# A transformer layer on one core: a later subtraction in the projection, and compression's first loads ahead of the phase boundary

## What is computed

```python
h = x * (1.0 + sc_m) + sh_m
q_a, kvc, kvs, kvw, g_a, p_b, q_c, k_c, v_c, g_mrg = _split(h @ lp['w_in'], IN_SPLITS)
kvc_full = jnp.concatenate([paged_rows(past['nsa_cmp'], past['page_table']), kvc], axis=3)
kc = compress_rows(kvc_full[:, 0], lp['phi_w1'][0], lp['phi_pe'][0], lp['phi_w2'][0])
def compress_rows(rows, w1, pe, w2):
    hid = lax.conv_general_dilated(rows, w1, (CMP_STRIDE,), 'VALID', ...)
    hid = jax.nn.gelu(hid + jnp.einsum('ld,ldh->h', pe, w1))
    return (hid @ w2).reshape(B, G, -1, dk)
```

## Time and profile before

| what | value |
|---|---|
| device time, median of 3 runs | 1933.16 us (1930.5 to 1934.42) |
| the profiled execution, own time | 1922.61 us |
| its span | 1920.8 us |
| TensorE busy | 1722.9 us (90%) |
| VectorE busy | 1100.5 us (57%) |
| ScalarE busy | 569.5 us (30%) |
| GpSimd busy | 425.6 us (22%) |

### The profile page before, as it was taken

One profiled execution on the slowest core, in us unless ns is written; L12 is line 12 of the kernel. 1 busy time (PEld: TensorE's weight loads), 2 busy tenths in 40 slices (PEclk: granted clock), 3 DMA queues, 4 the chain that ended last, 5 costly groups with the idle time before them and its releaser, 6 DMA issues. The chain is left out here.

```text
span 1920.8 us, 38852 instructions
## 1 busy us (share of the span) xinstructions
PE 1722.9 (90%) x16171; PEld 1506.5 (78%) x16171; DVE 1100.5 (57%) x1937; ACT 569.5 (30%) x1216; POOL 425.6 (22%) x525
## 2 busy tenths in 40 slices
PE   4999888988989995999998997777899999999998
PEld 1898778887988994999986454554797999999776
DVE  3214676677665433899974555364586544444456
ACT  1235433333222321343433665222553200000000
POOL 0000910000001303232312779544100000000500
PEclk7899999998999997999997999898999999999999
DMA  5547774353444766665653852567574233333231
GB/s 230 158 127 208 183 230 147 108 175 106 156 145 160 241 213 224 216 217 186 219 147 131 308 141 83 170 232 250 182 215 147 77 88 89 88 88 135 88 98 70
DMA packets 241285, 311.14 MB, mean 162 GB/s; under 512 B 41557, under 2 KB 192493, under 8 KB 235222
## 3 DMA queue, kind: packets, MB, share of 16 engines
q1 hardware_dynamic: 211862, 176.72, 30.0%
q0 software_dynamic: 29248, 131.93, 21.2%
HBM read 281.19 MB, written 79.61 MB: 188 GB/s over the span
## 5 line engine op out<-in xcount | busy, mean ns | idle before, releaser
L302 PE MATMUL inp_acc<-hh,inp_wh 128*128 128x272 f32 (+1 forms) x1072 | 340.1, 317 | 20.8 <-DVE inp_wl L274 18.8
L302 PE MATMUL inp_acc<-hl,inp_wh 128*128 128x272 f32 (+1 forms) x1072 | 316.2, 295 | 0.0
L302 PE MATMUL inp_acc<-hh,inp_wl 128*128 128x272 f32 (+1 forms) x1072 | 316.0, 295 | 0.0
L302 PEld LDWEIGHTS inp_acc<-hh,inp_wh 128*128 128x128 f32 (+1 forms) x1072 | 207.1, 193 | 36.2 <-DVE inp_wl L274 19.3
L274 DVE TENSOR_TENSOR inp_wl<-inp_w,inp_wh 128x1024 fp32r<-128x1024 f32 (+1 forms) x67 | 81.2, 1212 | 233.6 <-ACT inp_wh L455 233.2
L302 PEld LDWEIGHTS inp_acc<-hl,inp_wh 128*128 128x128 f32 (+1 forms) x1072 | 208.3, 194 | 3.4 <-issue 3.1
L302 PEld LDWEIGHTS inp_acc<-hh,inp_wl 128*128 128x128 f32 (+1 forms) x1072 | 207.6, 194 | 0.4
L563 POOL DMA_DIRECT2D out_dram<-in_cache_dil_dram x84 | 42.8, 514 | 519.2 <-PE inp_acc L302 498.5
L1410 PE MATMUL cmp_pH<-cmp_RTh,cmp_w1h 128*128 128x256 f32 (+1 forms) x512 | 150.1, 293 | 3.4 <-issue 3.4
L269 DVE CAST trk_wh<-trk_w 128x1024 fp32r<-128x1024 f32 x62 | 46.4, 749 | 180.3 <-PE trk_pz L283 124.2
L1410 PE MATMUL cmp_pH<-cmp_RTl,cmp_w1h 128*128 128x256 f32 (+1 forms) x512 | 147.2, 287 | 0.4 <-issue 0.4
(11 more groups left out here) (597 smaller groups left out, 3805.5 us busy)
## 6 DMA issues: line engine op xcount, KB each, us to landing
inp_w<-in_w_in_dram SPq DMA_DIRECT2D x66, 512.0 KB, 6.1
trk_w<-in_w_ffn_dram SPq DMA_DIRECT2D x66, 512.0 KB, 3.9
out_dram<-in_cache_dil_dram POOLq DMA_DIRECT2D x64, 511.0 KB, 5.5
sdi_kv<-in_cache_dil_dram SPq DMA_DIRECT2D x288, 64.0 KB
ringA<-in_w_ada_dram SPq DMA_DIRECT2D x16, 1024.0 KB, 7.5
PT<-inp_o SPq DMA_DIRECT2D x58, 272.0 KB, 4.7
ada_wada<-in_w_ada_dram SPq DMA_DIRECT2D x8, 1024.0 KB, 17.6
out_dram<-in_cache_dil_dram POOLq DMA_DIRECT2D x16, 508.0 KB, 8.2
```

What stands on the lines that cost most here:

```text
L302: i = pe.matmul(out, l, r, start=(first and n == 0), stop=(last and n == 2))
```

## The change

Three edits. (1) In the projection, DVE's low part of tile n stands at 2.5 eighths of tile n-1 in the plan, where it stood 0.4 eighths before it. This moves it for n from 15 on. (2) Page numbers, row indices, the first three work items' pages, the keys' first-stage weights and the position code are fetched inside the projection's block, into memory that the recurrence has left (`retired` waits until its last state steps are done). With this, cache piece 1 of the dilated scores goes behind the 24 small DMAs, and SP waits for the pages of work items 3 and 4 before these 24; clearing `sdi_new` on DVE goes behind the first low parts. (3) The position code is split into high and low parts as up to 4 extra columns of the first sequence's windows (256 to 259), so that `hidden(0)` and `hidden(2)` compute its product as columns 256 and 258; ACT copies that column into the bias. The 64 matmuls, two transposes and three DVE copies go.

```diff
     def vector(self, dve):
         for n, (c, t, rows) in enumerate(self.tiles):
-            yield self.at(n - 1, -0.4) if n else self.at(0) - 0.9
+            yield self.at(n - 1, 2.5) if n else self.at(0) - 0.9
...
+    def early_sync(self, sp):
+        yield -15
+        sp.dma_start(m["pages"][:, :], a["page_lanes"]).then_inc(m["pages_in"], 16)
+        sp.dma_start(m["lane"][:, :], a["c_lane"]).then_inc(m["pages_in"], 16)
+        yield start_of(5) + 18
+        self.retired(sp)
+        sp.dma_start(m["first_w1"][:, :, :], w1[:, 0]).then_inc(m["w1_in"], 16)
+        sp.dma_start(m["first_pe"][:, :], ...).then_inc(m["w1_in"], 16)
+    def early_vector(self, dve):
+        yield start_of(5) - 2
+        dve.wait_ge(m["pages_in"], 32)
...
+    def early_pool(self, pool):
+        yield start_of(5) + 19
+        self.retired(pool)
+        pool.wait_ge(self.m["pages_ready"], 4)
+        for w in range(3):
+            gather_pages(pool, self.a, self.m["pageidx"], self.m["first_pages"][:, (w + 2) % 4], self.m[f"got{w}"], 0, w)
...
-            nw = self.nwin(s) + 1
+            nw = 258 + w if w in (0, 2) else self.nwin(s) + 1
...
-            if w == 0:
-                yield 0.15
-                pe.wait_ge(self.pek, 1)
-                for v in range(2):
-                    pe.wait_ge(self.w1in[v], 16)
-                    for c in range(16):
-                        i = pe.matmul(pK[0:1, 0, v * P:(v + 1) * P], self.peT[:, v * 16 + c:v * 16 + c + 1], self.w1[:, v, c, :], ...)
...
         self.load(sp, 0)
-        self.load(sp, 1)
         sp.wait_ge(self.zeroed, 1)
+        for w in (3, 4):
+            sp.wait_ge(self.cmp.got[w], 32)
...
-        for i in range(2, len(self.order)):
+        for i in range(1, len(self.order)):
```

More of the change, by code:

```diff
@@ L587, in start_of, with gather_pages @@
     return PROLOGUE + ITER * t
+def gather_pages(pool, a, idx, dst, got, s, c):
+    src = a["cache_nsa_cmp"][0].rearrange("n v g (c l) d -> (n v g c) (l d)", l=16)
+    for h in range(2):
+        pool.indirect_dma_start(
+            out=dst[:, h, :], out_offset=None, in_=src,
+            in_offset=bass.IndirectOffsetOnAxis(ap=idx[:, c, 2 * s + h:2 * s + h + 1], axis=0),
+        ).then_inc(got, 16)
 class Mixer:
@@ L1312, in __init__ @@
         self.pK = ps("pK", [P, 2, 512])
-        (self.wfree, self.loaded, self.idx, self.ix, self.pet, self.pek, self.hcd, self.hck, self.turned, self.high,
+        (self.wfree, self.loaded, self.idx, self.ix, self.pet, self.pek, self.hck, self.turned, self.high,
          self.kept, self.hd, self.act, self.od, self.ok) = (sem(s) for s in (
[L1315 to L1318, removed]
+             "wfree", "loaded", "idx", "ix", "pet", "pek", "hck", "turned", "high", "kept", "hd", "act", "od", "ok"))
+        self.w1in = sem("w1in")
+        self.got = [m[f"got{i}"] if i < 3 else sem(f"got{i}") for i in range(self.NR)]
         self.gotp = [sem(f"gotp{i}") for i in range(2)]
@@ L1336, in pool @@
         a = self.a
-        src = a["cache_nsa_cmp"][0].rearrange("n v g (c l) d -> (n v g c) (l d)", l=16)
-        pool.wait_ge(self.idx, 5)
+        pool.wait_ge(self.idx, 1)
         for w, (s, c) in enumerate(self.work):
+            if w < 3:
+                continue
             if w >= self.NR:
                 pool.wait_ge(self.turned, self.read(w - self.NR))
[L1342 to L1349, removed]
+            gather_pages(pool, a, self.m["idx"], self.R(w), self.got[w % self.NR], s, c)
             if s == DB - 1:
@@ L1430, in tensor @@
         yield -0.5
[L1431 to L1432 removed]
+        pe.wait_ge(m["w1_in"], 32)
+        pe.transpose(pK[:, 0, 256:288], m["first_pe"][:, :], m["ident"][0:32, 0:32]).then_inc(self.pet, 1)
         for w in range(len(self.work)):
@@ L1447, in tensor @@
                 pe.wait_ge(self.wfree, w // 2 + 1)
+            if w == 0:
+                pe.wait_ge(self.pek, 1)
             hidden(w)
[L1449 to L1454, removed]
             yield w + 0.9
@@ L1488, in scalar @@
                 act.wait_ge(self.od, w - 1)
-            if w == 0:
-                act.wait_ge(self.hck, 1)
+            if w in (0, 2):
+                nc.scalar.activation(self.hc[:, w // 2:w // 2 + 1], self.pH[:, 0, 256 + w:257 + w], ACT.Copy).then_inc(self.hck, 1)
+                act.wait_ge(self.hck, w // 2 + 1)
             nc.scalar.activation(self.hid[:, w % 2, 0:self.nwin(s)], self.pH[:, w % 2, 0:self.nwin(s)], ACT.Gelu_apprx_tanh,
@@ L1500, in vector @@
     def vector(self, dve):
[L1501 removed]
+        m = self.m
         ch = Chain(dve, self.ix)
         yield -3
[L1504 to L1508, removed]
[L1509 to L1510 removed]
+        dve.tensor_copy(m["idx"][:, :, :], m["pageidx"][:, :, :]).then_inc(self.idx, 1)
         ch(dve.memset(self.zero[:, :], 0.0))
[L1512 to L1514 removed]
         def weights(v):
[L1517 to L1519 removed]
+            w1 = self.w1 if v else m["first_w1"][:, :, :]
+            if v:
+                dve.wait_ge(self.w1in, 16)
+            else:
+                dve.wait_ge(m["w1_in"], 32)
+            ch(split_high(dve, self.w1h[:, v], w1))
+            split_low(dve, self.w1l[:, v], w1, self.w1h[:, v]).then_inc(self.wfree, 1)
         def low(k, at, x):
@@ L3480 @@
 W0_AT = 224128
+PAGE_AT = 228608
+R_AT = 117056
+W1_AT = 177568
 def build(nc, a):
```

69 lines of the change are left out of this document (37 added, 32 removed).

## The result

| | before | changed |
|---|---|---|
| device time, median | 1931.83 us (4 runs, 1927.21 to 1934.42) | 1878.02 us (4 runs, 1871.16 to 1886.65) |
| the profiled execution, own time | 1922.61 us | 1879.86 us |
| its span, mean granted clock | 1920.8 us, 0.954 | 1878.0 us, 0.961 |

The ratio is 0.9726, with a 95% interval of 0.968 to 0.9772: faster. The time lies in the predicted range (1872 to 1914), 12 us under the predicted 1890 and 6 us above the range's lower end. Between the two profiled executions the difference is 42.8 us, where 43 were predicted; between the medians it is 53.8 us (with a fourth run of before, whose median was 1933.16 in three).

The account below looks back on a forecast made before the run. PE was taken as the bound, so gains must come from its gaps or clock. The later low part's 27 us plus the early loads' 16 us gave 43 us: 1933.2 - 43 = 1890 us, range 1872 to 1914.

Parts of the forecast that it names:

- Part 1: Projection beside the recurrence: a later DVE low part saves PE waits and clock dips; 27 us, bounds 8 to 42.
- The list of twelve waits: PE waits between 195.76 and 595.97 us whose producer stood behind a low part; they add up to 24.6 us.
- The 4 us for PE waiting on a late low part: Projection: deduction for places where PE would now wait for a low part that comes late; 4 us.
- the signs: Expected trace marks, among them DVE's `inp_wh` waits in projection from 157 to below 60 us, PE idleness from 50 to about 30.
- Part 2: Boundary to compression: first loads fetched ahead, during the projection; 16 us, between 8 and 24.
- the second chain: Compression's start: SP's queue and the 24 small DMAs' landing set DVE's first score product and PE's turn of item 4.
- the 762: Compression's start: predicted time of DVE's first score product, from SP's issue times plus 5.15 us landing; 777.66 before.
- Part 3: Compression's start: position code as columns removes 64 matmuls, 7.35 us, counted inside the early loads' gain.
- A: Projection: the later low part gives little, DVE being the slower engine in stretches; 24 us in all, 1909 us; chance 0.15.
- B: Compression's start: the small DMAs do not decide, landing earlier or DVE catching up; 51 us in all, 1882 us; chance 0.15.
- C: Projection: PE waits for the low part in each tile from 15 to 66; slower, 1940 us; chance 0.08.
- D: Boundary: early fetches delay last weights or stores, and the later low part gives little; no visible change, 1930 us; chance 0.07.

Follow-up runs that it names:

- the repeat: The changed kernel once more, no edit, in more rounds beside the kernel before: 1884.33 us, ratio 0.9754.
- The better version: Changed kernel with sample recurrence two units later, low part at 5.0, no page wait, first score product behind item 3's low parts: 1854.09 us, ratio 0.9602.

## Why the prediction was right, and what was off

**Part 1.** The mechanism is shown: the low part alone moves the projection's end and leaves compression as long as it was. In the pair of profiled executions it is 27.5 us against 27, and its make-up fits too: 19.9 us less idleness and 8.2 us less busy time at the higher clock, where three quarters of 24.6 and 11.9 are 18.5 and 8.9. But the medians give 33.6, and the step that was off is the sum's base: 43 us were worked out "against the profiled execution", and the 10.55 us between that execution and the median were carried along as a constant. That execution was an unusually good one: of the 46 runs of the kernel before on record only one was as fast (1920.99 us). Its compression (320.1) and the rest (882.1) are ordinary, so what was good about it was most likely the projection. The second profile of the old order took 583 us for that, not 569, but it was itself the slowest of its kernel's six runs. With the new order seven profiles (the changed kernel twice, and five kernels that keep its projection) end the stretch between 689.7 and 696.2. The mean of the two with the old order less the mean of these, 725.8 - 692.1 = 33.7, is what the medians say. So the new order probably also takes away waits and clock losses that the profiled execution of before by chance didn't have. Two profiles are few, one lucky and one unlucky; that the old order always scatters more is not shown. How far the base was off is open as well: the first runs say 53.8 us for the whole change, the repeat 47.4, and its interval (42 to 53) takes in the 43.

The list of twelve waits was right in kind: those for `rw_TT` went from 18.5 to 9.4 us. Not foreseen was the wait of 6.34 us for `rw_arb` at 244. DVE stands 7.09 us before an instruction of the sample recurrence, until the DMA of its start values has landed, and PE stands behind it. This pair was there before, smaller (DVE 4.16 us, PE 2.52 us, at 243), and the DMA's end is the same, 241.1 before and 241.2 after: both engines only come to it about 3 us sooner, and the low part, which now stands between the two DVE instructions, adds 1.2 us. Two units more for that recurrence gave 9 us. The 4 us for PE waiting on a late low part weren't needed; of the signs, DVE's waits fell to 67 us and not below 60.

**Part 2.** All signs came: first turn 5.0 us after the last projection matmul at a clock of 0.57 (696 to 700), `hidden(0)` 14.4 us after it (14 predicted), then 6.2 us of waiting at item 4 (6), and DVE 10.1 us for `sdi_new` (10). That the second chain decides was the riskiest step, and it is shown twice: 7.3 to 8.5 us of compression for 7.6 us of a later queue, and 10 us of matmuls put back for nothing. The gain of 16.5 us against 16 hides misses of the sum that partly cancel, and that is luck. The queue reached the end of the cache DMAs after 15.3 us and not 17.3. The wait for pages, which stood in the range but not in the 762, is 3.1 us, at its upper bound, because the pages landed 11.3 us after their issue and not 7.3, with the DMA engines at a share of 1.06 from 703 to 714. And the small DMAs landed 1.5 us after the last issue and not 5.15. Queue start to product: 38.1 predicted, 36.4 measured. What the sum left out is when POOL's page fetches run. Before, item 4's waited for DVE to have split the weights, which lay in the same memory, and so POOL issued the eight fetches of items 4 to 7 from 761.3 to 770.9, right ahead of the last small DMA (772.5); the 5.15 us were read there. With the change that wait is gone, and the fetches of items 3 to 7 are issued from 696.7 to 711.5: they keep the DMA engines busy during the wait for the pages, and are all issued 19 us before the last small DMA. With 1.05 us of page wait and 3.2 of landing in the repeat, and none and 3.6 without the wait, the two make about the same sum, 3.6 to 4.6 us: near this point they are no independent terms.

Of the two pages of the Trainium skill weighed there, the fixed cost of about 2 us per DMA (DMA: Bandwidth & Descriptors, Anatomy of one DMA) stands in a section on DMAs that GpSimd issues, and SP issues these; it is near the 1.5 us of this profile, but the repeat has 3.2. The rule on the shared port (SBUF — State Buffer, "SBUF: two separate sides") gave the right size for the page wait, but for another reason: only two of the four fetches ran beside the weight splitting (until 699.9) and were slow (1.67 and 2.02 us, the others 0.94), and the wait came from the landing.

**Part 3** was rightly left inside part 2: with the first loads ahead of the boundary it is worth nothing measurable here.

**The rivals.** A is out (27.5 to 33.6 us for the low part). B is out as a mechanism, though its 1882 is the nearest number. C is out at 2.5 eighths; it needs the low part almost at the tile's end. D is out: the early fetches delayed no store; the second item's turn waited 0.78 us, and not for a page.

**The better version.** The prediction named both stalls that were left (DVE's 10 us in front of the low parts of item 3) but priced them only as a consequence. Moving what waits behind what is ready gave 7.6 us, the same kind of edit as part 1.

## What to carry to other kernels

An engine with a fixed order should not hold ready work behind an instruction whose operand isn't there yet; look for such pairs in the longest groups of waits, and after each edit look for the next instruction that now comes too early. Work out the second chain (here a queue of small DMA issues and their landing) before pricing the first, since the later of the two sets the gain. Take the base of a sum from more than one execution: here a single one was 10.55 us better than the median, and the medians gave the edit 6 us more than that execution did.

## What the runs showed of the hardware

The time from the last of 24 issues of 8 KB to the release of the instruction that waits for them went with the load on the DMA engines (the last two columns are their share and GB/s; each window lies around the end of the last issue). Before, 5.15 us:

```profile
770.00:774.00 4.00, 2.67 (x17) 2.48 (x17) 1.06 (x2) 1.60 (x3) 1.59 (x2) 0.85 1.02 382
```

The changed kernel in its repeat, 3.2 us:

```profile
726.00:731.00 5.00, 4.79 (x37) 4.20 (x36) 0.00 (x0) 0.64 (x2) 0.87 (x1) 1.00 0.82 258
```

The changed kernel in its first profile, 1.5 us:

```profile
728.00:733.00 5.00, 3.13 (x24) 2.54 (x22) 0.47 (x1) 0.64 (x2) 0.00 (x0) 1.00 0.55 188
```

With the cache DMAs ahead it is 1.25 us, at a share of 0.06 from 741 to 745. Before, POOL's last page fetch ahead of the last small issue (772.5) is this one, with seven in a row ahead of it:

```profile
769.95 0.94 POOL L1346 DMA_INDIRECT cmp_R<-in_cache_nsa_cmp_dram,idx  x1 [0.30 <-issue]
```

The fourteen profiles fall into the same groups, by the share from 2 us before the end of the last issue until DVE's release: 5.0 and 5.15 us at 1.03 and 0.98, 2.6 to 3.7 us at 0.71 to 0.86 (eight profiles, among them the one without the wait for pages), 1.4 to 1.5 us at 0.43 to 0.48 (three), 1.2 us at 0.06. Within the group of eight the order is loose. The page fetches fit this too: in the eight, a pair of 512 KB fetches ends 1.0 to 2.0 us before the last small issue, in the three with 1.4 to 1.5 us 3.5 to 4.0 us before it, with 1.2 us 11 us before it. So a landing time read from one place holds for that load only, and two executions of one kernel differ by a factor of two. No run varied the page fetches by themselves: that landing, load and fetches go together is shown, that the fetches are the cause is argued.
